# A triangular inverse with even and odd columns apart, over 64 partitions, and 64-row products of b and k

## The reference

```
def step(state, inp):
    r_t, w_t, k_t, v_t, kk_t, a_t = inp
    sa = jnp.einsum('zbhvk,zbhk->zbhv', state, -kk_t)
    state = (state * w_t[..., None, :] + sa[..., :, None] * (kk_t * a_t)[..., None, :]
             + v_t[..., :, None] * k_t[..., None, :])
    y = jnp.einsum('zbhvk,zbhk->zbhv', state, r_t)
    return state, y
```

## Time and profile before

| what | value |
|---|---|
| median of three runs | 3403.81 us |
| the profiled execution | 3403.46 us |
| its span, first to last instruction | 3401.7 us |
| PE busy, share of the span | 3296.8 us, 97% |
| PE weight loads | 2727.4 us, 80% |
| VectorE (DVE) | 1846.6 us, 54% |
| ScalarE (ACT) | 1301.9 us, 38% |
| GpSimd (POOL) | 1578.1 us, 46% |

### The profile page before, as it was taken

One profiled execution on the slowest core, in us unless ns is written; L12 is line 12 of the kernel. 1 busy time (PEld: TensorE's weight loads), 2 busy tenths in 40 slices (PEclk: granted clock), 3 DMA queues, 4 the chain that ended last, 5 costly groups with the idle time before them and its releaser, 6 DMA issues.

```text
span 3401.7 us, 42068 instructions
## 1 busy us (share of the span) xinstructions
PE 3296.8 (97%) x15943; PEld 2727.4 (80%) x15943; DVE 1846.6 (54%) x2336; ACT 1301.9 (38%) x2131; POOL 1578.1 (46%) x1492
## 2 busy tenths in 40 slices
PE   7999999999889999999899999999999999999998
PEld 6788878788578888888578878888888888888886
DVE  3665655555666777664432023456456456455556
ACT  4534344444155665663342232233233233223222
POOL 4554533333258888886365433333333323323323
PEclk9999999999899999999899999999999999999999
DMA  5444453433355555554543323332332333323323
GB/s 170 129 142 141 142 154 116 120 112 90 91 143 136 148 135 140 125 128 122 201 143 113 123 75 100 118 106 87 112 99 88 117 93 104 107 87 111 111 81 106
DMA packets 666051, 405.06 MB, mean 119 GB/s; under 512 B 193534, under 2 KB 597178, under 8 KB 665338
## 3 DMA queue, kind: packets, MB, share of 16 engines
q1 hardware_dynamic: 665850, 402.38, 40.8%
HBM read 347.05 MB, written 54.53 MB: 118 GB/s over the span
## 4 chain that ended last, share of the span: by engine, by line
PE 49%; DVE 1%; ACT 0%; issue 0%; POOL 0%; DVEq 0%; ACTq 0%; POOLq 0%
PE f_bank L2194 9%; PE f_bank L2195 9%; PE f_bank L2196 9%; PE f_bank L2232 4%; PE f_bank L2233 4%; PE f_bank L2234 4%; PE f_bank L2172 2%; PE f_bank L2174 2%; PE f_bank L2173 2%; PE f_bank L2115 1%; PE f_bank L2116 1%; PE f_bank L2117 1%; PE f_bank L2124 0%; PE f_bank L2150 0%; DVE orw_plain L2688 0%
## 5 line engine op out<-in xcount | busy, mean ns | idle before, releaser
L2483 POOL TENSOR_TENSOR w_lo_b<-w_raw_b,w_hi_b 128x1024 fp32r<-128x1024 f32 x176 | 435.7, 2479 | 903.9 <-ACT w_hi_b L2359 903.7
L2194 PE MATMUL f_bank<-act_rounded,w_lo_b 128*128 128x512 f32 x1408 | 549.3, 390 | 1.2 <-DVE act_rounded L2595 1.2
L2195 PE MATMUL f_bank<-act_rounded,w_hi_b 128*128 128x512 f32 x1408 | 548.0, 389 | 0.0
L2196 PE MATMUL f_bank<-act_rounded,w_hi_b 128*128 128x512 f32 x1408 | 547.9, 389 | 0.0
L1294 POOL TENSOR_TENSOR ring_w_rounded<-ring_w_plain,ring_w_hi 128x1024 fp32r<-128x1024 f32 x134 | 327.3, 2447 | 463.1 <-ACT ring_w_hi L1310 463.0
L1622 PE MATMUL slab_ps<-h_hi,ring_w_rounded 128*128 128x512 f32 x1056 | 426.2, 404 | 2.7 <-DVE h_lo L1451 2.4
L1623 PE MATMUL slab_ps<-h_lo,ring_w_hi 128*128 128x512 f32 x1056 | 414.6, 393 | 0.0
L1624 PE MATMUL slab_ps<-h_hi,ring_w_hi 128*128 128x512 f32 x1056 | 414.1, 392 | 0.0
L2359 ACT CAST w_hi_b<-w_raw_b 128x1024 fp32r<-128x1024 f32 x176 | 185.0, 1052 | 452.9 <-DMA w_raw_b<-in_w_ffn_up_dram 207.1
L2194 PEld LDWEIGHTS f_bank<-act_rounded,w_lo_b 128*128 128x128 f32 x1408 | 264.7, 188 | 56.0 <-DVE act_rounded L2595 1.1
L2196 PEld LDWEIGHTS f_bank<-act_rounded,w_hi_b 128*128 128x128 f32 x1408 | 264.5, 188 | 55.1
(11 more groups left out here) (432 smaller groups left out, 6234.7 us busy)
## 6 DMA issues: line engine op xcount, KB each, us to landing
ring_w_plain<-in_w_in_dram SPq DMA_DIRECT2D x190, 512.0 KB, 4.1
w_raw_b<-in_w_ffn_gate_dram SPq DMA_DIRECT2D x88, 512.0 KB, 3.7
w_raw_b<-in_w_ffn_up_dram SPq DMA_DIRECT2D x88, 512.0 KB, 3.7
w_raw_b<-in_w_ffn_down_dram SPq DMA_DIRECT2D x42, 512.0 KB, 4.1
w_raw_b<-in_w_out_dram SPq DMA_DIRECT2D x16, 1024.0 KB, 5.1
zt<-slab_out SPq DMA_DIRECT2D x63, 256.0 KB, 4.3
hid_plain<-in_w_ffn_down_dram SPq DMA_DIRECT2D x21, 512.0 KB, 4.5
oa_plain<-in_w_ffn_down_dram SPq DMA_DIRECT2D x21, 512.0 KB, 4.3
```

What stands on the lines that cost most here:

```text
L2194: pe.matmul(o, wl[:, k, :], act_hi[:, kk, :], start=kk == 0, stop=False)
L2195: pe.matmul(o, wh[:, k, :], act_lo[:, kk, :], start=False, stop=False)
L2196: return pe.matmul(o, wh[:, k, :], act_hi[:, kk, :], start=False, stop=stop)
L2483: pool.tensor_tensor(low(r), slab_raw(j % 2), high(r).bitcast(F32), ALU.subtract).then_inc(slab_low, 1)
```

## The change

- The inverse. Rows and columns of the 32 x 32 blocks are sorted by parity, even tokens first, and POOL works on 64 partitions for 32, the two halves of which hold the even and the odd columns of the inverse (`inv`, 16 columns for each row). Both halves need all of the block, so each block is loaded twice. The result is no longer made in place: `inv` is cleared and its diagonal set by three memsets, and then there are 31 steps with two operations each, of 2 x k x n elements a partition.
- SP issues eight transfers for blocks where there were four, and eight for d_bd in each direction where there were four, each of 32 partitions x 4 rows x 16 elements for 32 x 4 x 32.
- "ab" and "ak" become one stage "abk": for each pair and each head a product over that head's 64 partitions only, with b and k side by side as weights (128 columns) and a and r as the moving side, into one bank for each head. Eight products, where there were four and four. b_bd, k_bd and ScalarE's "bd" go.
- VectorE masks with new masks, which it builds at the start of the scan from three iotas of POOL. The mask operations work on one half of the partitions at a time: "n" (two), "ab" (two), "ak" (four) where there were one, one and three. The store of n_sb waits for "n".
- "operands" writes a by parity (two operations of half the size), b by parity (likewise), r twice (into `var` and `xar`), and k; a goes to `var` without its sign, the copy to av goes, and ScalarE puts the sign in with its scale.

The diff, cut to its core:

```diff
-GATE_SHARE = {"ab": 2, "ak": 2, "av": 3, "bk": 3, "akv": 3, "ts": 3}
-DVE_SLOT = (("ab", "v"), ("xadd", "u"), ("ak", "v"), ("decays", "w"), ("qg", "u"), ("operands", "w"), ("state", "u"))
+GATE_SHARE = {"abk": 2, "lx": 3, "av": 2, "bk": 3, "akv": 3, "ts": 3}
+DVE_SLOT = (("n", "v"), ("xadd", "u"), ("ab", "v"), ("ak", "v"), ("decays", "w"), ("qg", "u"), ("operands", "w"), ("state", "u"))
...
+                tok = qg[:, 0:2, :].rearrange("p a n -> p (a n)")
+                for i, (base, pat) in enumerate(((0, [[HALF, 2], [1, 2], [2, EVERY]]), (HALF, [[-HALF, 2], [1, 2], [2, EVERY]]), (0, [[1, CH]]))):
+                    pool.iota(tok[:, i * CH:(i + 1) * CH], base=base, pattern=pat, channel_multiplier=0,
+                              allow_small_or_imprecise_dtypes=True).then_inc(tokens_made, 1)
+                for t in (ak_bd, w_bd, u_bd, *d_bd):
                     pool.memset(t[:, :, :], 0.0).then_inc(zeroed, 1)
                 for t in low:
                     pool.memset(t[:, :, :], 0.0).then_inc(zeroed, 1)
                 for t in v_t:
                     pool.memset(t[:, :, :], 0.0).then_inc(zeroed, 1)
+                done = 0
                 for it in range(NUNIT // 2):
-                    m = blocks[it % 2]
-                    step = both_steps[HALF * (it % 2):HALF * (it % 2) + HALF, :]
-                    pool.wait_ge(n_landed[it % 2], 64 * (it // 2 + 1))
-                    done = it * 61
-                    pool.memset(m[:, :, :].rearrange("p i t -> p (i t)")[:, 0:HALF * HALF:HALF + 1], 1.0).then_inc(inv_chain, 1)
+                    m, x, step = blocks[it % 2], inv[it % 2], steps[it % 2]
+                    if it >= 2:
+                        pool.wait_ge(inv_stored[it % 2], 16 * (it // 2))
+                    pool.memset(x[:, :, :], 0.0).then_inc(inv_chain, 1)
                     done += 1
-                    for j in range(HALF - 2, 0, -1):
-                        n = HALF - 1 - j
-                        shape = [HALF, j, n]
-                        st = step[:, 0:j * n].rearrange("p (i t) -> p i t", t=n)
-                        pool.tensor_tensor(st, m[:, 0:j, j:j + 1].broadcast_to(shape), m[:, j:j + 1, j + 1:HALF].broadcast_to(shape),
-                                           ALU.mult).then_inc(inv_chain, 1)
+                    pool.wait_ge(inv_chain, done)
+                    flat = x[:, :, :].rearrange("p i c -> p (i c)")
+                    for r in range(2):
+                        pool.memset(flat[r * HALF:(r + 1) * HALF, r * EVERY * EVERY:(r + 1) * EVERY * EVERY:EVERY + 1], 1.0).then_inc(inv_chain, 1)
+                    done += 2
+                    pool.wait_ge(inv_chain, done)
+                    pool.wait_ge(n_landed[it % 2], 128 * (it // 2 + 1))
+                    rows = lambda t: t.rearrange("p (r c) n -> p r c n", r=2)
+                    for j in range(HALF - 1, 0, -1):
+                        k, n, c, at = (j + 1) // 2, EVERY - j // 2, j // 2, (j % 2) * EVERY + j // 2
+                        shape = [CH, 2, k, n]
+                        st = step[:, 0:2 * k * n].rearrange("p (r i n) -> p r i n", r=2, n=n)
+                        pool.tensor_tensor(st, rows(m)[:, :, 0:k, at:at + 1].broadcast_to(shape),
+                                           x[:, at:at + 1, c:EVERY].unsqueeze(1).broadcast_to(shape), ALU.mult).then_inc(inv_chain, 1)
                         pool.wait_ge(inv_chain, done + 1)
-                        pool.tensor_tensor(m[:, 0:j, j + 1:HALF], m[:, 0:j, j + 1:HALF], st, ALU.add).then_inc(inv_chain, 1)
+                        pool.tensor_tensor(rows(x)[:, :, 0:k, c:EVERY], rows(x)[:, :, 0:k, c:EVERY], st, ALU.add).then_inc(inv_chain, 1)
...
-                        sp.wait_ge(taken_dve, DVE_AT["ab", v])
+                        sp.wait_ge(taken_dve, DVE_AT["n", v])
                         sp.dma_start(nb[it % 4, s].rearrange("q p t -> p q t"), n_sb[:, :, :]).then_inc(n_stored, 16)
                         if s == 1:
                             sp.wait_ge(n_stored, 16 * (v + 1))
                             if it >= 2:
-                                sp.wait_ge(inv_stored[it % 2], 16 * (it // 2))
+                                sp.wait_ge(inverted, it - 1)
                             for z in S2:
                                 src = nb[it % 4, z].rearrange("q (e i) t -> (q e) i t", e=2)
                                 for hb in range(2):
-                                    at = 8 * (2 * hb + z)
-                                    sp.dma_start(blocks[it % 2][at:at + 8, :, :],
-                                                 src[:, hb * HALF:(hb + 1) * HALF, hb * HALF:(hb + 1) * HALF]).then_inc(n_landed[it % 2], 16)
+                                    for r in range(2):
+                                        at = r * HALF + 8 * (2 * hb + z)
+                                        sp.dma_start(blocks[it % 2][at:at + 8, :, :],
...
-                                    sp.dma_start(d_bd[s][at:at + HALF, :, at:at + HALF], src[e]).then_inc(d_landed[s], 16)
+                                for r in range(2):
+                                    at = r * HALF + 8 * (2 * hb + s)
+                                    src = yb[it % 2, at:at + 8, :].rearrange("(q e) (i t) -> e i q t", e=2, t=EVERY)
+                                    for e in range(2):
+                                        at = CH * e + HALF * hb
+                                        sp.dma_start(d_bd[s][at:at + HALF, :, at + r * EVERY:at + (r + 1) * EVERY], src[e]).then_inc(d_landed[s], 16)
                             for e in range(2):
-                                at = CH * e
-                                sp.dma_start(low[s][at:at + HALF, :, at + HALF:at + CH],
-                                             nb[it % 4, s, :, at:at + HALF, HALF:CH].rearrange("q i t -> i q t")).then_inc(d_landed[s], 16)
+                                first, last = CH * e + HALF * s, CH * e + HALF * (1 - s)
+                                sp.dma_start(low[s][first:first + HALF, :, last:last + HALF],
+                                             nb[it % 4, s, :, first:first + HALF, last - CH * e:last - CH * e + HALF].rearrange("q i t -> i q t")
+                                             ).then_inc(d_landed[s], 16)
                     for h in next_halves(slot + 1)[1:]:
...
+                tok = qg[:, 0:2, :].rearrange("p a n -> p (a n)")
+                dve.wait_ge(tokens_made, 3)
+                masks_done = [0]
+
+                def in_turn(ins, n=1):
+                    ins.then_inc(masks_made, 1)
+                    masks_done[0] += n
+                    dve.wait_ge(masks_made, masks_done[0])
+                row = [qg[:, 2, i:i + 1] for i in range(3)]
+                for i in range(3):
+                    in_turn(dve.tensor_tensor(qg[:, 3, 0:CH], tok[:, i * CH:(i + 1) * CH], g.eyes[:, :], ALU.mult))
+                    in_turn(dve.tensor_reduce(row[i], qg[:, 3, 0:CH], AX.X, ALU.add))
+                for i in range(2):
+                    place_a, natural = tok[:, i * CH:(i + 1) * CH], tok[:, 2 * CH:3 * CH]
+                    dve.tensor_scalar(masks[0][i][:, :], place_a, row[i], -1.0, ALU.is_gt, ALU.mult)
+                    dve.tensor_scalar(masks[1][i][:, :], natural, row[i], None, ALU.is_ge)
+                    in_turn(dve.tensor_scalar(masks[2][i][:, :], place_a, row[2], -1.0, ALU.is_gt, ALU.mult))
                 eyes = g.eyes[:, :].unsqueeze(1).broadcast_to([P, NQ, CH])
                 def low_part(h, q):
...
+                            dve.wait_ge(made, PE_AT["abk", n])
                             if n >= 1:
                                 dve.wait_ge(n_stored, 16 * n)
-                            dve.tensor_tensor(n_sb[:, :, :], bank[1][:, :, 0:CH], strict, ALU.mult)
-                            dve.tensor_tensor(rb[st][:, :, 0:CH], bank[1][:, :, CH:P], within, ALU.mult).then_inc(taken_dve, 1)
+                            for e in range(2):
+                                r = slice(CH * e, CH * e + CH)
+                                ins = dve.tensor_tensor(n_sb[r, :, :], bank[1 + 2 * e][0:CH, :, 0:CH], mask_ba[s][0:CH], ALU.mult)
+                            ins.then_inc(taken_dve, 1)
+                        elif name == "ab":
+                            for e in range(2):
+                                r = slice(CH * e, CH * e + CH)
+                                ins = dve.tensor_tensor(rb[st][r, :, 0:CH], bank[1 + 2 * e][0:CH, :, CH:P], mask_br[s][0:CH], ALU.mult)
+                            ins.then_inc(taken_dve, 1)
                         elif name == "xadd":
                             dve.wait_ge(made, PE_AT["lx", n])
                             dve.tensor_tensor(xar[st][:, :, 0:P], xar[st][:, :, 0:P], bank[2][:, :, :], ALU.add).then_inc(taken_dve, 1)
                         elif name == "ak":
-                            dve.wait_ge(made, PE_AT["ak", n])
                             for e in range(2):
```

(74 more changed lines are left out.)

38 lines of the change are left out of this document (17 added, 21 removed).

## The result

The changed kernel takes 3428.0 us, median of 5 runs (3420.56 to 3433.95), where the one before took 3404.6 beside it (3403.66 to 3404.89): a ratio of 1.007, 95% interval 1.0058 to 1.0081. I had forecast 3401 with a range to 3419. It is slower, and by more than the range allowed. The profiled execution took 3424.74 us (span 3423.0, 21.3 over the span before).

The account below looks back on a forecast made before the run. A ring paced by POOL's 39 us inversion bounds the scan, then SP's issues would; first inverse -2.7, 13 pairs +6.5, last inverse -6.6 sum to -2.8 us: 3403.8 - 2.8 = 3401 us, range 3384 to 3419.

Parts of the forecast that it names:

- SP's ring in POOL's place: Middle of the scan: SP's issues, v_in, VectorE and yh set the pace, not POOL's inversion; +0.5 us a pair.
- A pair then: Pair of scan slots: v_in +0.9, mask result +0.3, VectorE -0.7, together +0.5 us; +6.5 in 13 pairs.
- The descriptors in a transfer are as many as before, half as long.: SP's loads of blocks and d_bd: issue cost per transfer unchanged; +1.5 us for blocks, +3.7 for d_bd.
- Rival B: SP's queue costs more, landings slow and VectorE contention doesn't fall: +1.5 us a pair, 3414 us; chance 0.11.
- -4.3 +1.5 +0.3 = -2.5: Terms ahead of d_bd in a pair: SP's wait for POOL -4.3 us, blocks' issues +1.5, mask result +0.3.
- The inversion: POOL's inverse in the scan: about 32 us, for 39 in the middle before; 64 partitions as free as 32.
- SP's wait for POOL: SP's wait for the inverse in the scan, 82.9 us over 16 times, goes: -4.3 us a pair.
- The products abk: Sixteen PE passes with both halves together, about 1.0 us; saves 0.4 us of PE a unit, mask result +0.3.
- Rival A: The abk halves run one after the other: a pair costs +1.3 us, 3412 us, slower; chance 0.24.
- First inverse: Start of the scan: start +3.0 us later, inversion -7.6, d_bd +1.9, together -2.7; PE still waits some 8.
- Last inverse: End of the scan: PE's wait of 4.0 us and the low clock behind it go, together -6.6 us.
- Rival C: PE sets the pace if half-size issues cost half: up to 1.5 to 2 us a pair, 3373 us; chance 0.19.

Follow-up runs that it names:

- a8_filler: The changed kernel with eight throwaway products on TensorE right before yh waits for qg in even slots: 3416.0 us, for 3428.0.
- b2_cut_transfers: The kernel before, with each load of blocks and d_bd cut into two of half the columns, same bytes: +0.6% (20 us) over the kernel before.
- a10_blocks_once: The changed kernel without the second copy of blocks (four loads a pair, not eight; result not the reference's): 1.3% (45 us) under the changed kernel.
- a6: The changed kernel with yb stored by POOL's own queue and the odd unit's d_bd and low behind the next inputs' loads: 3376.6 us, 0.9939 of before.
- a9: The changed kernel with yb stored by POOL on its own queue, not by SP: 0.9% (29 us) under the changed kernel.

## Why the prediction was wrong

It forecast +0.5 us for a pair and 2.0 came, in 14 pairs; that is 22 of the 24 us between the forecast sum (-2.8) and the longer span (+21.3). The mechanism, SP's ring in POOL's place, was right. Two terms stood in the sum at nothing without a reason: the low clock behind yh's wait, and the landing of yb behind twice the bytes of blocks.

*The low clock.* The step that failed is "*A pair then*: +0.9 +0.3 -0.7 = +0.5 us over now". It takes the stretch from yh to the next odd x1 as it was. By the means of 13 pairs yh came 0.9 us later (+31.7 to +32.6), near the 0.5 of the sum, but from yh to the next odd x1 it was 8.7 us for 7.4. I gave the low clock a price at the last pair (2.5 us) and none in the middle, where it cost 17 us of the scan. yh's wait grew from 0.7 to 2.5 us: 0.9 by yh's being late, and some 0.8, an estimate from TensorE's own work of a pair (below), since TensorE gets there with less work (the gate tiles ahead of yh are as many as before, ten of a slot's sixteen shares). a8_filler agrees: with the same lateness and the wait filled, the pair is 1.0 us over the kernel before and not 2.0. Whether the saving on TensorE alone would have brought the low clock is not shown; b2_cut_transfers has no such saving, waits of 2.2 us and 10.2 us of low clock.

*The blocks.* The other step is "The descriptors in a transfer are as many as before, half as long." For d_bd it holds. For blocks each transfer is as long as before, and there are twice as many: the bytes double. I priced the issues (+1.5; measured 3.11 for 1.50 us) and nothing behind them. The median landing of yb went from 1.9 to 4.2 us (the mean of 13 pairs from 2.2 to 4.0), and the first inverse began 5.8 us later, not 3.0. a10_blocks_once shows what it is worth: without the second copy and its four issues the same kernel is 45 us faster, and faster than the one before. Rival B had "also slows the landings" in it, with 1.5 us a pair and 3414; that was the right place with too small a size. The list of transfers with their KB, multiplied out for the diff, would have shown it.

*Luck.* d_bd comes 2.6 us earlier (+15.3 to +12.7), where the sum has -4.3 +1.5 +0.3 = -2.5, though yb's landing took 1.8 us that the sum lacks. Another miss hid it: the blocks are issued at +5.1 for +6.7, forecast 0.3 later, mostly since the store of nb lands in 2.0 us for 3.4. In the kernel before SP had issued a load of gate weights (512 KB) 1.0 to 2.5 us ahead of that store in 10 of the 13 pairs, in the changed kernel in one. That fits the slow yb behind its blocks, but no run tests it.

*The inversion*: forecast 32 us, measured 32.3 (1218.6 to 1250.9); 64 partitions cost nothing, 120 elements take 461 ns where the line of the earlier trace rows gives 477. Right. *SP's wait for POOL*: 11.1 us are left of 82.9, none of it in the middle, as said. But -4.3 a pair was no gain of the inversion: b2 shows that it goes with any other pace.

*The products abk*: sixteen passes take 1.10 us at 1249.28, forecast about 1.0. 512 of them are busy 38.1 us where ab and ak had 69.1 for as many; the two halves run together. The rule of the Trainium skill ("TensorE: Matmul & The Clock Gate", Part 3) on products in different row groups agrees with this. Rival A is out. TensorE's own work of a pair, the pair less waits and low clock, is 36.7 us (41.3 less 2.5, 0.8 and 1.3) for 37.5: 0.8, the forecast 0.4 for each of two units.

*VectorE*: cum to the end of qg took 3.99 us (1235.04 to 1239.03) for 4.70: -0.71 for -0.7. *d_bd*: eight take 3.87 us undisturbed, 4.81 right behind yb; forecast 3.6 to 3.7.

*First inverse*: -2.7 forecast, +0.6 measured. The blocks are issued 2.1 us later (971.07 to 973.14; forecast 1.5), and take 7.4 us to POOL's start for 3.6 (forecast +1.5, for the issues). The inversion took 33.6 for 41.1, as forecast, and d_bd its 1.9 more. TensorE waited 11.4 us there, not the 8 that were left in the forecast. *Last inverse*: -6.6 forecast, -4.4 measured; the wait of 4.0 us before the second last even x1 is 0.95 and has no low clock behind it. *After the scan*: 0 in the sum, -3.9 measured; the low clock costs 5.1 less there.

*Rival C* (TensorE sets the pace) was nearly the state that a6 reached, not this change: there d_bd of the odd unit is out of the way of v_in, and POOL stores yb. Of its pair 0.9 us are waits.

## What to carry to other kernels

Multiply out the bytes of every transfer that a diff touches, not only its count; then ask what is queued behind it. When one link of a ring is shortened, compute the ring without the wait for that link first: what another link then adds is all that counts, and order on the queue can be worth more than the engine's time. A wait of two microseconds on TensorE may cost nearly as much again (1.7 us or 3.4 behind nine of thirteen waits here); keep the work that can be moved in front of the place where it waits.

## What was not expected of the hardware

The low clock doesn't follow each wait: after 1.95 us at 1239.13 it fell until 1242.8, and after 3.34 us at 1527.87 it didn't.

How long a store of 128 KB takes to land depends on what else was issued near it. In the changed kernel the fourteen stores of yb right behind the blocks (0.4 to 1.1 us after the last) land in 3.3 to 4.7 us; with half the bytes ahead of them (a10) all but the last land in 2.2 to 2.6. Being behind them in the same queue isn't needed, as POOL's stores in a9 show (3.1 to 4.4 us near the blocks, 2.3 to 2.4 far from them). The DMA engines were fully busy (share 1.01) from 1231 to 1239, so that transfers wait for each other there is likely, but no run shows it. Blocks aren't the only cause: in the kernel before two stores of yb, 4.7 and 5.0 us after the last blocks, took 3.2 and 3.6.
